# Gathering the rows of two expert pairs at once, with single-pass products, in a mixture of experts on one core

## What is computed

```
def hierarchical_moe(h, w_rg, b_rg, w_re, b_re, w_gate, w_up, w_down):
    t = h.reshape(-1, d)
    g_prob = jax.nn.softmax((t @ w_rg + b_rg).astype(f32), axis=-1)
    ...
    top_l, top_i = lax.top_k(e_in, TOP_K)
    ...
    for e in range(N_EXPERTS):
        hid = jax.nn.silu(t @ w_gate[e]) * (t @ w_up[e])
        out = out + gates[:, e:e + 1] * (hid @ w_down[e])
    return out.reshape(b, s, d)
```

## Time and profile before

| what | value |
|---|---|
| median of 3 runs | 1680.19 us (1678.5 to 1682.64) |
| the profiled execution | 1683.05 us, of which the span is 1681.3 us |
| granted TensorE clock, mean | 0.986 |
| TensorE busy | 95% of the span |
| mean rate of the DMAs over the span | 198 GB/s |

### The profile page before, as it was taken

The page is one execution under the profiler, slowest core; times in us unless marked ns, Lnnn a source line. Parts: engine busy times, 40 slices in busy tenths (PEclk is TensorE's granted clock), DMA queues, the critical chain, the costliest instruction groups (busy, mean ns, idle before and its releaser), DMA issues.

```text
span 1681.3 us, 22363 instructions
## 1 busy us (share of the span) xinstructions
PE 1595.3 (95%) x9359; PEld 1239.7 (74%) x9359; DVE 939.9 (56%) x1374; ACT 653.9 (39%) x960; POOL 27.1 (2%) x89
## 2 busy tenths in 40 slices
PE   5999999999999889899999999999999999999998
PEld 1998655454445378687888899988768878889986
DVE  3876666642222265565685666545466567556653
ACT  2543410111111243565644543435365744543441
POOL 1000010100000000000000000000000000000000
PEclk9999999989999989999999999999999999999999
DMA  8555518889989924423354455545424235435651
GB/s 306 189 186 200 202 51 292 328 360 412 413 356 423 390 99 149 126 96 109 145 177 153 143 172 188 200 150 193 153 76 151 101 126 182 169 122 192 201 178 73
DMA packets 153090, 333.33 MB, mean 198 GB/s; under 512 B 17699, under 2 KB 69157, under 8 KB 140709
## 3 DMA queue, kind: packets, MB, share of 16 engines
q1 hardware_dynamic: 147440, 326.94, 53.7%
q10 hardware_dynamic: 5558, 5.06, 0.9%
HBM read 330.94 MB, written 1.05 MB: 197 GB/s over the span
## 4 chain that ended last, share of the span: by engine, by line
PE 80%; DVE 8%; DMA 6%; ACT 4%; issue 1%; POOL 0%; ACTq 0%; POOLq 0%; DVEq 0%; SPq 0%
PE ps_g L737 19%; PE ps_g L718 16%; PE ps_g L1142 6%; PE ps_g L1282 6%; PE ps_s L1538 4%; PE ps_p L1538 3%; PE ps_o L785 3%; PE ps_g L878 3%; DMA arena<-in_w_up_dram 3%; PE ps_p L718 2%; DVE ring_r L2292 2%; DMA ring<-in_w_mod_dram 2%; PE ps_s L718 1%; PE ps_x L691 1%; PE ps_o L1171 1%
## 5 line engine op out<-in xcount | busy, mean ns | idle before, releaser
L2292 DVE TENSOR_TENSOR ring_r<-ring,late_w 128x4096 fp32r<-128x4096 f32 (+1 forms) x50 | 216.9, 4339 | 153.6 <-ACT late_w L1854 153.6
L1854 ACT ACTIVATE late_w<-ring 128x4096 fp32r<-128x4096 f32 (+1 forms) x50 | 178.1, 3563 | 127.9 <-PE ps_p L1538 42.8
L737 PE MATMUL ps_g<-hf_high,ring_r 128*128 128x256 f32 x640 | 178.8, 279 | 0.0
L737 PE MATMUL ps_g<-hf_high,late_w 128*128 128x256 f32 x576 | 162.1, 281 | 0.0
L737 PE MATMUL ps_g<-h_t_r,late_w 128*128 128x256 f32 x576 | 161.2, 280 | 0.0
L737 PEld LDWEIGHTS ps_g<-hf_high,ring_r 128*128 128x128 f32 x640 | 121.9, 190 | 0.0
L737 PEld LDWEIGHTS ps_g<-h_t_r,late_w 128*128 128x128 f32 x576 | 108.6, 189 | 0.0
L737 PEld LDWEIGHTS ps_g<-hf_high,late_w 128*128 128x128 f32 x576 | 108.1, 188 | 0.0
L1878 ACT ACTIVATE arena<-arena,neg_max 128x256 f32<-128x256 f32 (+1 forms) x160 | 71.5, 450 | 40.7 <-DVE neg_max L2347 40.7
L1142 PE MATMUL ps_g<-arena 128*64 128x512 f32 x288 | 85.9, 599 | 0.0
L718 PE MATMUL ps_g<-early_w,first_low 128*128 128x512 f32 (+1 forms) x176 | 68.7, 391 | 3.7 <-ACT arena L1840 1.8
(11 more groups left out here) (697 smaller groups left out, 3713.6 us busy)
## 6 DMA issues: line engine op xcount, KB each, us to landing
ring<-in_w_in_dram SPq DMA_DIRECT2D x31, 2048.0 KB, 7.8
ring<-in_w_gate_up_dram SPq DMA_DIRECT2D x44, 1024.0 KB, 7.2
arena<-in_w_down_dram SPq DMA_DIRECT2D x16, 2048.0 KB, 13.5
ring<-in_w_mod_dram SPq DMA_DIRECT2D x10, 2048.0 KB, 10.3
ring<-in_w_down_dram SPq DMA_DIRECT2D x10, 2048.0 KB, 8.0
arena<-in_w_up_dram SPq DMA_DIRECT2D x8, 2048.0 KB, 17.7
ring<-in_w_gate_dram SPq DMA_DIRECT2D x8, 2048.0 KB, 14.5
ring<-in_w_up_dram SPq DMA_DIRECT2D x4, 2048.0 KB, 18.3
```

The source lines that it names most:

```text
L737: ins = pe.matmul(b.ap[:, (f % 2) * SEQ:(f % 2 + 1) * SEQ], a[:, k, f * P:(f + 1) * P], x[:, k, :], start=k == 0 and i == 0, stop=k == nk ...
L1854: act.activation(high_of(name, rnd)[:, 0:n], ring[:, slot, 0:n], ACT.Copy).then_inc(high_ready.sem, 1)
L2292: dve.tensor_tensor(ring_r[:, slot, 0:n], ring[:, slot, 0:n], high_of(name, rnd)[:, 0:n].bitcast(F32), ALU.subtract).then_inc(low_ready.se ...
```

## The change

The gathers for pairs q + 2 and q + 3 are made together, behind the odd pair q + 1. For that `h_rows` is split once into a high part (four pieces, copied by ScalarE) and a low part (subtracted by VectorE, in place over `h_rows`), both of type fp32r, whose products run in a single pass. `gather_two` does 32 such products of 256 columns in place of two times 16 f32 products of 128 columns. An even pair has no gather in it any more. Since the pairs 0 and 1 have no odd pair ahead of them, both are gathered ahead of the loop, in the old way (`first_gather`), and the split is made behind that. Half of the gathered rows now stands in `h_t`, so `pair_low` moves out of it into a place of its own. ScalarE and VectorE loop over two pairs at a time too. The order and the waits of the transfers stay: for each block SyncE waits for the same products as before.

```diff
-        taken_t = view(at + D, KD, P)
+        taken_t = view(at + D, KD // 2, SEQ), h_t[:, KD // 2:, :]
...
-            def gather(q, name="taken"):
-
-                pe.wait_ge(pick_ready, q + 1)
+            def first_gather(p):
+
+                pe.wait_ge(pick_ready, p + 1)
                 for j, b in enumerate((MO, MX)):
-                    claim(b, name, q - 1)
+                    claim(b, f"taken{p}")
                     for i in range(4):
                         k = 4 * j + i
                         for tb in range(TB):
-                            ins = pe.matmul(b.ap[:, i * P:(i + 1) * P], h_rows[:, tb, k * P:(k + 1) * P], pick[:, tb, :],
+                            ins = pe.matmul(b.ap[:, i * P:(i + 1) * P], h_rows[:, tb, k * P:(k + 1) * P], pick_r[:, tb, p * P:(p + 1) * P].bitcast(F32),
                                             start=tb == 0, stop=tb == TB - 1)
                     ins.then_inc(b.full, 1)
+
+            def gather_two(q):
+
+                pe.wait_ge(routed_low_ready, len(ROUTED_PIECES))
+                pe.wait_ge(pick_ready, q + 4)
+                for r in range(2):
+                    for j, b in enumerate((MO, MX)):
+                        claim(b, f"taken{r}", q)
+                        for i in range(2):
+                            for tb in range(TB):
+                                for part in range(2):
+                                    ins = pe.matmul(b.ap[:, i * SEQ:(i + 1) * SEQ], routed(part, tb, 4 * r + 2 * j + i), pick_r[:, tb, :],
+                                                    start=tb == 0 and part == 0, stop=tb == TB - 1 and part == 1)
+                        ins.then_inc(b.full, 1)
...
-            gather(0, "taken")
+            for p in range(2):
+                first_gather(p)
...
-                if not last:
-                    gather(q + 1)
+                if odd and not last:
+                    gather_two(two)
...
+            for piece, (tb, lo, n) in zip(routed_high, ROUTED_PIECES):
+                act.activation(piece[:, :], h_rows[:, tb, lo * P:(lo + n) * P], ACT.Copy).then_inc(routed_high_ready, 1)
             act.wait_ge(route_in, 1)
             act.activation(rt_s[:, 1], rt_s[:, 0], ACT.Exp).then_inc(route_out, 1)
...
-            dve.wait_ge(MX.full, MX.nth("start", "taken"))
-            def pair_vectors(q, last=False):
-                dve.wait_ge(MX.full, q * 2 + 1)
-                if not last:
-                    pick_slots(q + 1, pick, False).then_inc(pick_ready, 1)
+            dve.wait_ge(MX.full, MX.nth("start", "taken1"))
+            dve.wait_ge(routed_high_ready, len(ROUTED_PIECES))
+            for piece, (tb, lo, n) in zip(routed_high, ROUTED_PIECES):
+                cols = slice(lo * P, (lo + n) * P)
+                dve.tensor_tensor(routed_low[:, tb, cols], h_rows[:, tb, cols], piece[:, :].bitcast(F32), ALU.subtract).then_inc(routed_low_ready, 1)
+            def pair_vectors(q, odd, last=False):
+                if not odd and not last:
+                    dve.wait_ge(MX.full, q * 2 + 2)
+                    for p in range(2):
+                        pick_slots(q + 2 + p, pick_r[:, :, p * P:(p + 1) * P], False).then_inc(pick_ready, 1)
```

More of the change, by code:

```diff
@@ L1131, in weights_of @@
                     return up_w[e]
-                for b in (MO, MX):
-                    pe.wait_ge(b.free, q * 2 + 1)
+                two = q - odd
+                if not odd:
+                    for b in (MO, MX):
+                        pe.wait_ge(b.free, two * 2 + 2)
                 claim(M0, "gate", q)
@@ L1167, in expert_pair @@
                     if not last:
-                        claim(y, "out", q)
+                        claim(y, ("out_even", "out_odd")[odd], two)
                     for k in range(KF):
@@ L1187, in _ @@
                 even_and_odd(q)
-            for b in (M0, M1, MO, MX):
+            for b in (M0, M1):
                 b.again()
@@ L1659, in _ @@
                          **{f"up{e}": (M1.full, lambda q: M1.nth("moe", "up", q)) for e in range(2)},
-                         **{f"down{e}": (MX.full, lambda q: MX.nth("moe", "out", q)) for e in range(2)}}
+                         **{f"down{e}": (MX.full, lambda q, odd: out_count(MX, q, odd)) for e in range(2)}}
             def load_gates(p, q, after):
@@ L1691, in load_rest @@
                     where, count = done_with[name]
-                    sync.wait_ge(where, count(q - 1))
+                    sync.wait_ge(where, count(q - 1, (p - 1) % 2) if name.startswith("down") else count(q - 1))
                     load_expert(name, p)
@@ L2044, in pair_scalars @@
                 act.activation(pick_t[:, 0, :], M1.ap[:, 0:SEQ], ACT.Copy).then_inc(M1.free, 1)
[L2045 to L2046 removed]
+                if odd and not last:
+                    take_two(q - 1)
                 for half, b in enumerate((MO, MX)):
                     cols = slice(half * HALF, (half + 1) * HALF)
[L2049 removed]
+                    act.wait_ge(b.free, out_count(b, q, odd, last))
                     act.activation(pair_high[:, cols], pair_y[:, 0, cols], ACT.Copy).then_inc(pair_high_ready, 1)
[L2052 to L2054 removed]
+            with act.Fori(0, last_even, 2) as q:
+                for odd in range(2):
+                    pair_scalars(q + odd, odd)
+            for odd in range(2):
+                pair_scalars(last_even + odd, odd, last=True)
             for l in range(LAYERS):
@@ L2917, in pair_vectors @@
                 dve.wait_ge(M1.full, M1.nth("moe", "turned", q))
-                if not last:
+                if not (odd and last):
                     pick_slots(q + 1, pick_g, True).then_inc(pick_g_ready, 1)
@@ L2926, in pair_vectors @@
                     dve.tensor_tensor(pair_low[:, cols], pair_y[:, 0, cols], pair_high[:, cols].bitcast(F32), ALU.subtract).then_inc(pair_low_ready, 1)
-            with dve.Fori(0, last_pair) as q:
-                pair_vectors(q)
-            pair_vectors(last_pair, last=True)
+            with dve.Fori(0, last_even, 2) as q:
+                for odd in range(2):
+                    pair_vectors(q + odd, odd)
+            for odd in range(2):
+                pair_vectors(last_even + odd, odd, last=True)
             dve.sem_inc(last_used, 1)
```

77 lines of the change are left out of this document (47 added, 30 removed).

## The result

| what | before | changed |
|---|---|---|
| median | 1682.4 us (1678.5 to 1683.45, 6 runs) | 1689.89 us (1688.48 to 1692.35, 6 runs) |
| ratio to before | | 1.0043, 95% interval 1.0031 to 1.0056 |
| the profiled execution, and its span | 1683.05, 1681.3 us | 1689.78, 1688.0 us |

The change costs 7.5 us, where +1.4 was forecast. The time lies above the range.

A forecast was written before the change was run, and what follows sets the result against it. The mixture of experts was taken as a relay of TensorE and transfer-queue legs; 3.68 - 0.75 - 1.49 = +1.4 us gave 1684.5 us against the profiled execution, 1681.6 against the median, range 1675 to 1686.5.

The forecast's parts named there:

- The first leg: TensorE until pair 2's gate weights are issued (366.32 us): a second gather ahead of the loop adds 3.68 us.
- Copies of the split: Four ScalarE copies, starting costs some 2.4 us, fit into 4.85 us of idle time: 0 us.
- The second leg: Queue from issue of pair 2's gate weights to landing of pair 3's `up1`, 83.95 us: a thin place filled, -0.75 us.
- The third leg: TensorE from pair 3's `up1` landing to pair 4's down products' end: gather saved, odd gather dearer, clock fall; -1.49 us.
- whether the queue still runs empty: Before pair 5's down weights: queue empty at 496.9 or 498.6 us, pair 4's down products ending at 500.2; answered yes.
- The fourth and fifth legs: Queue from pair 5's down weights' issue to pair 7's `up1` landing, 63.6 us, then TensorE to the end: 0 us.
- the two falls of the forecast: Granted clock falls behind the waits for `up1` of pairs 3 and 7; 1.69 us added for pair 3, pair 7's already there.
- a leg of the queue: A stretch of the stage paced by transfers: TensorE's savings within it only lengthen its waits at the landings.

The follow-up runs named there:

- The repeat of before: The kernel before, unedited, measured and profiled once more: 1681.46 us, ratio 0.9994.
- the repeat: The changed kernel, unedited, measured and profiled once more: 1687.57 us, ratio 1.0035 to the kernel before.
- before, new order: Kernel before, down weights of odd pairs sent behind the next pair's gate weights, `up1` behind the next pair's `up0`: 1678.91 us, ratio 0.998.
- before, light queue: Kernel before, only half of `up1`, `down0` and `down1` transferred for pairs 1 to 7: 1677.28 us, ratio 0.9975.
- changed, light queue: Changed kernel, only half of `up1`, `down0` and `down1` transferred for pairs 1 to 7: 1668.75 us, ratio 0.9921 to the kernel before.
- before, first gather twice: Kernel before, the first gather's 16 products issued twice ahead of the loop: 1685.24 us, ratio 1.002.
- changed, new order: Changed kernel, down weights of odd pairs sent behind the next pair's gate weights, `up1` behind the next pair's `up0`: 1681.28 us, ratio 0.9989.
- changed, half of down(4): Changed kernel, only half of pair 4's two blocks of down weights transferred: 1684.3 us, ratio 1.0012 to the kernel before.
- changed, gates first at p = 4: Changed kernel, gate and `up0` weights of pair 5 issued ahead of `up1` of pair 4: 1685.89 us, ratio 1.0016 to the kernel before.
- changed, second gather cut: Changed kernel, pair 1's gather ahead of the loop cut from 16 products to 2: 1686.1 us, ratio 1.0021 to the kernel before.
- changed, gather of two cut: Changed kernel, each gather for two pairs cut from 32 products to 4: 1688.44 us, ratio 1.0037 to the kernel before.
- changed, gates first at p = 5 too: Changed kernel, gate and `up0` weights of pairs 5 and 6 issued ahead of `up1` of pairs 4 and 5: 1692.49 us, ratio 1.0062.

## Why the prediction was wrong

*The first leg, +3.68:* right. Between the two first profiles it is +3.60, with one fall of the clock in each: before it lies in the first gather (3.65 us), in the changed kernel in the gate and up products of pair 0 (15.60 us instead of 13.95). The repeat of before has 13.28, since no fall of the clock lay in it, which makes the mean +4.3. The doubled gather in the kernel before gave +3.0 in the median.

*Copies of the split at nothing:* right. The four copies took 2.19 us (from 340.54, for the forecast's 2.4), and ScalarE was still idle for 3.44 us before the exponential at 346.17. The chain ahead of the loop holds no row of them.

*The second leg, -0.75:* right (-0.43 between the first two profiles, -1.1 between the means). The wait at `up1` of pair 3 was forecast at 7.2 us. It was 5.6 us, and 1.8 us had already been waited at `up1` of pair 2.

*The third leg, -3.27 + 0.09 + 1.69 = -1.49:* **this is the step that failed.** The terms are about right. The gather of two pairs took 3.89 us for 3.77. An even pair has 1.22 us from its transposes to its down products (380.21 to 381.43), where I had 1.40. The clock fell behind the landing, 8.60 for 7.09. What is wrong is the claim that this leg is TensorE's, with nothing put down for a wait on a transfer in it: the queue sets it. I asked whether the queue still runs empty before the down products of pair 4 end, and it does. I did not ask when the last blocks that come ahead of that emptiness land. They are pair 4's own down weights. In the kernel before, theirs is the eighth block behind the landing at 450.27 (two of down(3), `up1` of 4, two of gates, `up0` of 5, two of down(4)), and 8 x 5.1 us later is some 491 (an estimate), against a need at 491.71. There was nothing to spare, and the 3.27 us that the even pair saves could not be had. It came worse: `up1` of pair 4 is issued when the up products of pair 3 are done, and these ended 8.7 us behind the landing and not 7.2 as before, behind the fall of the clock. The two blocks that were then in the queue should land 10.2 us behind 454.84, at 465.0, and the windows show their last bytes some 2 us earlier, at 462 to 464; the transfer issued at 463.61 shows at 464 to 466. In between the queue was nearly dry. From the issue at 463.61 to the landing at 496.10 are 32.5 us, six blocks and the start. Then 0.24 + 3.65 + 3.43 us of TensorE, and the leg is 48.62. So the clock's fall reaches this leg through the late issue of `up1` of pair 4. In the repeat the leg is 51.28: the up products of pair 3 took 9.51 us instead of 8.60, and a fall behind the new wait itself made the down products 5.35 us instead of 3.65, together 2.6 us. That pair 4's down weights set the leg is shown by the experiment with half of them: 46.90.

*The fourth and fifth legs, 0:* right for the fourth (-0.2; TensorE waited 4.6 us there, for the 5.0 forecast). In the fifth the fall of the clock behind the wait isn't always there: 21.65 and 20.22 us before, 21.63 and 21.43 changed. The 20.22 holds a wait of 0.8 us for pair 7's own down weights, which land close to their need too.

*The clock:* 1.69 us is the right size for one fall. In the first profile of the changed kernel the stage has, behind the first leg, the two falls of the forecast (454 and 567 us). In the repeat it has more, and over all runs the changed kernel lost more than that. The profiles show the loss in portions of 1.7 us, at places that vary from run to run. Counted over all timed runs as (1 - granted clock) x span, which is a mean of three-digit clocks and so coarse:

| kernel | TensorE's waits for transfers in the stage, us | mean time lost to the clock, us |
|---|---|---|
| before, new order | 0 | 19.0 |
| before, light queue | 0 | 20.0 |
| changed, light queue | 0 | 18.7 |
| before (two measurements) | 3.7, 4.8 | 20.0, 19.9 |
| before, first gather twice | 4.2 | 19.2 |
| changed, new order | 10.2 | 21.7 |
| changed, half of down(4) | 12.0 | 23.3 |
| changed, gates first at p = 4 | 12.1 | 24.8 |
| changed (two measurements) | 14.0, 13.9 | 27.9, 23.2 |
| changed, second gather cut | 14.0 | 26.5 |
| changed, gather of two cut | 13.7 | 30.6 |
| changed, gates first at p = 5 too | 16.1 | 27.1 |

TensorE waits 10 us more in the changed kernel, and loses 3 to 8 us more to the clock. The two go together only roughly: the kernel before loses as much with no wait in the stage (light queue) as with 4 or 5 us, and the unedited changed kernel lost 27.9 us in one measurement and 23.2 in the other. No run sets the clock apart from the waits, so that one causes the other is not shown. I had taken waits within a leg of the queue to cost nothing ("only makes these waits longer"). The two profiles of the changed kernel have falls behind two waits (454 and 567 us) and at three (449 to 455, 493 and 565). The Trainium skill, "TensorE: Matmul & The Clock Gate", section on HAM oscillation, describes a kernel in which TensorE waits for a transfer long enough for its clock to fall, so that the next group of matmuls starts at the low clock. The traces agree at these places (granted clock 0.50), and not every wait has it: behind the 1.8 us at `up1` of pair 2 the products took 7.11 us. Not every lost microsecond counts, since a fall inside a leg of the queue is paid out of the wait.

*What stays open:* the stage accounts for 5.1 us of a difference that was 7.5 in one measurement and 5.8 in the other. Between 620 and 1600 us, far behind the stage, the profile of the changed kernel has falls at 710 and 1205 us and its repeat at 708 and 828; that of before has one at 1361, and its repeat two, at 1238 and 1358. Whether the change moves these or they are scatter, four profiles don't tell. The difference ahead of the stage (1.4 us, 351.60 and 353.00 at its start) isn't there in the repeats (349.08 and 349.40).

*Sizes:* the forecast's 1681.6 was missed by 8.3 us. The stage, +5.1 us instead of +1.4, is 3.6 of them. Some 2.2 are the reference: the median of before was 1680.19 in three runs and 1682.4 in six. The rest, 2.5, is what stays open.

## What to carry to other kernels

When a queue and an engine take turns at setting the pace, it is not enough to find where the queue runs empty. For each block find the distance between its landing and its first use, with and without the saving. A saving on the engine is worth no more than the smallest of these distances on the way (here about nothing, at the down weights of pair 4), and here more waiting for transfers went with more time lost to the clock. A change that shortens the engine's work should come with a new order of the transfers: the order alone gave -3.8 us on the kernel before, and 6 to 9 us on the changed one. But where the queue's own total is as long as the engine's, no order lets the saving through: with the new order in both, the changed kernel stayed 2.4 us behind. To price an experiment that leaves work out, look in its profile for what took the place of that work: in two of these a wait for another engine took part of it.

## What the hardware showed that I had not expected

TensorE's clock fell in equal portions: in windows of 1 us over all fourteen profiles the shortest stretches of granted clock 0.50 cost 1.7 us each, and the longer ones 3.4, 5.1 or 6.8, all but the one at the very end of the program. The kernel before lost between 13 and 27 us to it from one run to the next, and its times scatter over some 9 us: of one set of runs, the shortest (1679.0 us) had lost 13.4 and the longest (1687.3) 27.0. Kernels whose TensorE never waits for a transfer in the stage still lost 19 to 20 us in the mean over the whole program.
